# Mixture-of-experts loop on one core: a shared TensorE block for 64 and 96 rows, the 128-row body set apart, the split item reordered, the second weight sum made before an expert's early items

## The reference, cut to what matters

```python
def expert_block(args):
    e, tok, gt = args
    xb = hf[tok]
    g = xb @ w_gate[e] + b_gate[e]
    u = xb @ w_up[e] + b_up[e]
    g = jnp.minimum(g, SWIGLU_LIMIT)
    u = jnp.clip(u, -SWIGLU_LIMIT, SWIGLU_LIMIT)
    act = (u + 1.0) * (g * jax.nn.sigmoid(g * SWIGLU_ALPHA))
    y = act @ w_down[e] + b_down[e]
    return y * gt[:, None].astype(y.dtype)
```

## Time and profile before

| | us |
|---|---|
| median of three runs (lowest, highest) | 2254.84 (2250.0, 2255.2) |
| the profiled execution's own time | 2249.11 |
| its span, first to last instruction | 2247.3 |
| TensorE matmul busy | 2097.6 |
| VectorE busy | 1229.5 |
| ScalarE busy | 647.5 |
| mean granted TensorE clock | 0.975 |

### The profile page before, as it was taken

How to read it: one execution, slowest core, us unless ns; L and a number is a source line. 1 busy time by engine, 2 the same in 40 slices (tenths; PEclk the granted TensorE clock), 3 DMA queues, 4 the chain that set the end, 5 groups by cost and what they waited for, 6 DMA issues and landing times.

```text
span 2247.3 us, 35366 instructions
## 1 busy us (share of the span) xinstructions
PE 2097.6 (93%) x11374; PEld 911.6 (41%) x11375; DVE 1229.5 (55%) x2403; ACT 647.5 (29%) x1252; POOL 567.1 (25%) x537
## 2 busy tenths in 40 slices
PE   8999999977999799899898999979998999999997
PEld 6546676433333333333333334323332333333343
DVE  4323996776573563277263546526643576556753
ACT  2001886122322332222223232212222222222332
POOL 3271124133221221221222213211212122122223
PEclk9999999988999899999999999989999999999998
DMA  8002000246688569389859667765889868677674
GB/s 308 20 16 88 28 1 6 90 167 239 223 286 313 186 224 323 125 288 325 318 172 338 241 244 246 247 240 181 306 297 352 306 226 284 226 248 246 234 253 183
DMA packets 151941, 485.70 MB, mean 216 GB/s; under 512 B 20288, under 2 KB 37973, under 8 KB 151310
## 3 DMA queue, kind: packets, MB, share of 16 engines
q1 hardware_dynamic: 116192, 444.81, 52.5%
q0 software_dynamic: 33792, 34.66, 8.1%
q10 hardware_dynamic: 1874, 5.02, 0.6%
HBM read 461.26 MB, written 43.09 MB: 224 GB/s over the span
## 4 chain that ended last, share of the span: by engine, by line
PE 89%; issue 4%; DVE 2%; ACT 2%; DMA 1%; POOL 1%; DVEq 1%; ACTq 0%; POOLq 0%
PE psum L2283 24%; PE psum L2312 15%; PE psum L2079 14%; PE psum L1718 6%; PE psum L2125 5%; PE psum L1824 4%; PE psum L1857 3%; PE psum L1817 3%; PE psum L1714 2%; PE psum L2005 2%; PE psum L2066 2%; PE psum L2137 1%; PE psum L1866 1%; PE psum L2307 1%; PE psum L2290 1%
## 5 line engine op out<-in xcount | busy, mean ns | idle before, releaser
L774 POOL DMA_INDIRECT residual_rows<-work x184 | 330.5, 1796 | 584.5 <-ACT work L994 534.4
L2312 PE MATMUL psum<-weights,work 128*128 128x512 f32 x736 | 326.8, 597 | 26.0 <-ACT work L1024 26.0
L2079 PE MATMUL psum<-weights,work 128*64 128x512 f32 (+2 forms) x1536 | 308.3, 607 | 36.0 <-issue 36.0
L2283 PE MATMUL psum<-x,work 128*64 128x512 f32 x1472 | 331.7, 598 | 3.6 <-DVE work L1554 3.6
L1547 DVE TENSOR_TENSOR x<-weights 128x2048 f32<-128x2048 f32 x92 | 206.7, 2289 | 112.0 <-PE psum L2290 73.9
L2283 PE MATMUL psum<-weights,work 128*64 128x512 f32 x1104 | 250.6, 596 | 0.0
L731 POOL DMA_INDIRECT work<-normed_rows,work x47 | 51.6, 1098 | 713.1 <-PE psum L2005 520.9
L1404 DVE SCALAR_TENSOR_TENSOR work<-psum,work 128x4 f32<-128x4 f32 x47 | 7.4, 158 | 402.3 <-PE psum L1998 402.3
L2312 PEld LDWEIGHTS psum<-weights,work 128*128 128x128 f32 x736 | 136.2, 190 | 189.5 <-issue 189.5
L1547 DVE TENSOR_TENSOR x<-weights,x 128x2048 f32<-128x2048 f32 x92 | 208.2, 2284 | 0.4 <-DMA weights<-in_w_up 0.4
L2079 PEld LDWEIGHTS psum<-weights,work 128*64 128x64 f32 (+2 forms) x1536 | 97.6, 133 | 226.1 <-issue 223.9
(11 more groups left out here) (302 smaller groups left out, 2694.0 us busy)
## 6 DMA issues: line engine op xcount, KB each, us to landing
weights<-in_w_gate SPq DMA_DIRECT2D x64, 2048.0 KB, 8.0
weights<-in_w_up SPq DMA_DIRECT2D x64, 2048.0 KB, 13.6
weights<-in_w_down SPq DMA_DIRECT2D x64, 2048.0 KB, 8.6
residual_rows<-x SPq DMA_DIRECT2D x9, 512.0 KB, 2.9
normed_rows<-work ACTq DMA_DIRECT2D x9, 512.0 KB, 2.8
x<-in_x SPq DMA_DIRECT2D x8, 512.0 KB, 9.0
weights<-in_w_in SPq DMA_DIRECT2D x16, 256.0 KB, 9.3
weights<-in_w_in SPq DMA_DIRECT2D x8, 512.0 KB, 11.8
```

Of the source, the lines that this page charges most:

```text
L774: pl.indirect_dma_start(acc_d[:, :], bass.IndirectOffsetOnAxis(dest[:, b:b + 1], 0), yrow[:, b * BLK:(b + 1) * BLK], None, bounds_check=UN ...
L2079: mm = pe.matmul(out.rearrange("p (m n) -> p m n", m=2), xT[:, k, lo:lo + cols], wgu[:, :, k, blk * BLK:(blk + 1) * BLK], start=(k == 0), ...
L2283: mm = pe.matmul(out, tokens[:, k, :], weights[:, :, k, g * BLK:(g + 1) * BLK], start=start and k == 0, stop=ends and k == 3)
L2312: mm = pe.matmul(bank(4 + h), actT[:, k, :], wdn[:, k, h * HALF:(h + 1) * HALF], start=False, stop=(k == DT - 1))
```

## The change

On TensorE the bodies for 64 and 96 rows are cut in three: a first part of each (its waits, for 96 rows the third unit's first half, and `own_places`), then a common block `experts_halves` (both halves of units 0 and 1, the next rows, `index`, biases), then an end of each. The body for 128 rows is emitted ahead of `experts_next`, outside the stretch of the loop's other blocks. In the split item the bias of bank 3 starts its group instead of ending it, in both places; `transposes(2)` goes ahead of `row_transposes(1)`; `transposes(3)` goes ahead of the fourth pair of down products. On VectorE `weight_sum(1)` moves from the split item to the expert's start, behind `weight_sum(0)`, with its wait for `s_wk[1]`.

```diff
@@ -1580,10 +1580,6 @@
...
                 split_token_sum(3)
-                dve.wait_ge(s_wk[1], 32 * e + 32)
-                dve.wait_ge(s_wts, 8 * n + (WTS0 + 2))
-                weight_sum(1, 0)
-                weight_sum(1, 1)
                 dve.wait_ge(s_prod, 3 * n + 2)
@@ -1625,6 +1621,11 @@
...
                     weight_sum(0, 1)
+                    n = dve.value_load(splits[0:1, bass.ds(e, 1)], min_val=0, max_val=EXPERTS)
+                    dve.wait_ge(s_wk[1], 32 * e + 32)
+                    dve.wait_ge(s_wts, 8 * n + (WTS0 + 2))
+                    weight_sum(1, 0)
+                    weight_sum(1, 1)
                 run_early(begin, stop)
@@ -2000,10 +2001,10 @@
...
-                for c in range(4):
-                    k = 4 * q + c
-                    mm = pe.transpose(bank(7, P, c * P), xg[:, k * P:(k + 1) * P], ident[:, :])
-                mm.then_inc(s_xtp, 1)
+                all_four = [pe.transpose(bank(7, P, c * P), xg[:, (4 * q + c) * P:(4 * q + c + 1) * P], ident[:, :])
+                            for c in range(4)]
+                all_four[-1].then_inc(s_xtp, 1)
+                return all_four
@@ -2083,18 +2081,18 @@
...
-                    for s in range(1 if tokens == 32 else 2):
-                        mm = pe.transpose(bank(6, P, s * P), hid[:, b, s * P:(s + 1) * P], ident[:, :])
-                    return mm
+                    return [pe.transpose(bank(6, P, s * P), hid[:, b, s * P:(s + 1) * P], ident[:, :])
+                            for s in range(1 if tokens == 32 else 2)]
...
-                    if tokens in (64, 96):
+                    if tokens == 64:
...
-                            mm = pe.matmul(PS[64 * h:64 * h + 64, 4 * HALF:5 * HALF], onesb[rows_of(h), 0:64],
-                                           brow_dn[rows_of(h), :], start=True, stop=False)
+                            pe.matmul(PS[64 * h:64 * h + 64, 4 * HALF:5 * HALF], onesb[rows_of(h), 0:64],
+                                      brow_dn[rows_of(h), :], start=True, stop=False)
+                        return
@@ -2175,14 +2173,11 @@
...
-                units = 2 if tokens == 32 else {64: 2, 96: 3, 128: 4}[tokens]
-                pe.wait_ge(s_xT, 2 * j + 1)
-                pe.wait_ge(s_wk[0], 32 * e + 32)
-                pe.wait_ge(s_hid, UNIT * j + UNIT)
-                pe.wait_ge(s_aTm, UNIT * j + 1)
-                for b in range(units):
-                    mm = gate_up(b, range(4))
-                mm.then_inc(s_k03, 1)
+                def item_waits():
+                    pe.wait_ge(s_xT, 2 * j + 1)
+                    pe.wait_ge(s_wk[0], 32 * e + 32)
+                    pe.wait_ge(s_hid, UNIT * j + UNIT)
+                    pe.wait_ge(s_aTm, UNIT * j + 1)
@@ -2190,74 +2185,104 @@
...
-                    row_transposes(q)
...
+                    return row_transposes(q)
...
+                def place_waits():
+                    pe.wait_ge(s_idxb, j + 2)
+                    pe.wait_ge(s_found, 2 * j + 2)
...
+                def bias_waits():
+                    pe.wait_ge(s_chosen, j + 1)
+                    pe.wait_ge(s_yr, UNIT * j + UNIT)
...
+                def gate_up_ends(b, last=False):
+                    gate_up(b, range(4, DT)).then_inc(s_gu, UNIT - b if last else 1)
...
+                def hidden(b, last=False):
+                    transposes(b)[-1].then_inc(s_htp, UNIT - b if last else 1)
...
+                def next_item():
+                    pe.reg_load(next_tokens, items[0:1, bass.ds(j + (TABLE + 1), 1)])
+                    pe.reg_load(loaded_expert, items[0:1, bass.ds(j + 1, 1)])
+                    pe.reg_alu(next_expert, loaded_expert, 0, ALU.max)
+                    pe.reg_load(third_expert, items[0:1, bass.ds(j + 3, 1)])
...
+                if part == "places":
+                    item_waits()
+                    if tokens == 96:
+                        gate_up(2, range(4))
+                    place_waits()
+                    own_places()
+                    return
+                if part == "halves":
+                    gate_up(0, range(4))
+                    gate_up(1, range(4)).then_inc(s_k03, 1)
+                    rows(0)
+                    bias_waits()
+                    index(j + 2)
+                    bias(0)
+                    bias(1)
+                    down_bias()
+                    pe.wait_ge(s_wk[1], 32 * e + 32)
+                    gate_up_ends(0)
+                    gate_up_ends(1)
+                    return
+                if tokens == 64:
+                    next_item()
+                    next_rows()
+                    both = transposes(0)
+                    both[0].then_inc(s_gu, UNIT - 2)
+                    both[1].then_inc(s_htp, 1)
+                    rows(1)[0].then_inc(s_biased, 1)
+                    down_64(0, 0)
+                    hidden(1, True)
+                    down_64(0, 1)
+                    down_64(1, 0).then_inc(s_d03, 1)
+                    down_64(1, 1).then_inc(s_dps, 1)
+                    return
+                if tokens == 96:
+                    bias(2)
+                    down_bias()
+                    next_rows()
+                    hidden(0)
+                    gate_up_ends(2, True)
+                    next_item()
+                    hidden(1)
+                    rows(1)
+                    down_64(0, 0)
+                    down_64(0, 1)
+                    hidden(2, True)
+                    down_64(1, 0)
+                    down_64(1, 1)
+                    down_rest().then_inc(s_dps, 1)
+                    return
...
+                units = 2 if tokens == 32 else UNIT
+                item_waits()
+                for b in range(units):
+                    mm = gate_up(b, range(4))
+                mm.then_inc(s_k03, 1)
...
-                pe.wait_ge(s_aTm, UNIT * j + 1)
-                pe.wait_ge(s_idxb, j + 2)
-                pe.wait_ge(s_found, 2 * j + 2)
-                pe.wait_ge(s_chosen, j + 1)
-                pe.wait_ge(s_yr, UNIT * j + UNIT)
+                place_waits()
+                bias_waits()
...
-                def gate_up_ends(b):
-                    gate_up(b, range(4, DT)).then_inc(s_gu, 1 if b < units - 1 else UNIT - b)
...
-                def hidden(b):
-                    transposes(b).then_inc(s_htp, 1 if b < units - 1 else UNIT - b)
...
-                def next_item():
-                    pe.reg_load(next_tokens, items[0:1, bass.ds(j + (TABLE + 1), 1)])
-                    pe.reg_load(loaded_expert, items[0:1, bass.ds(j + 1, 1)])
-                    pe.reg_alu(next_expert, loaded_expert, 0, ALU.max)
-                    pe.reg_load(third_expert, items[0:1, bass.ds(j + 3, 1)])
...
+                gate_up_ends(0)
+                gate_up_ends(1, tokens == 32)
...
-                    gate_up_ends(0)
-                    gate_up_ends(1)
...
-                    hidden(1)
+                    hidden(1, True)
...
@@ -2284,11 +2309,11 @@
...
-                def bias(to, h, ends):
+                def bias(to, h, first):
...
-                                       start=False, stop=ends)
+                                       start=first, stop=not first)
@@ -2324,7 +2349,8 @@
...
-                bias(1, 0, True).then_inc(s_prod, 1)
+                bias(1, 0, False).then_inc(s_prod, 1)
+                bias(3, 1, True)
@@ -2332,8 +2358,8 @@
...
                 for k in range(4):
-                    product(3, a12, wgt_half(1, 1), k, True, False)
-                bias(3, 1, True).then_inc(s_gu, 1)
+                    mm = product(3, a12, wgt_half(1, 1), k, False, True)
+                mm.then_inc(s_gu, 1)
@@ -2357,13 +2383,12 @@
...
                 pe.wait_ge(s_yr, UNIT * j + UNIT)
+                pe.wait_ge(s_u, 7 * n + (UNIT0 + 1))
                 for h in range(2):
-                    mm = pe.matmul(bank(4 + h), onesb[rows_of(h), :], brow_dn[rows_of(h), :], start=True, stop=False)
-
-                pe.wait_ge(s_u, 7 * n + (UNIT0 + 1))
-                summed(3, 3, a22, True, False)
-                bias(3, 1, True).then_inc(s_gu, 1)
-                pe.sem_inc(s_biased, 1)
+                    pe.matmul(bank(4 + h), onesb[rows_of(h), :], brow_dn[rows_of(h), :], start=True, stop=False)
+                bias(3, 1, True).then_inc(s_biased, 1)
+
+                summed(3, 3, a22, False, True).then_inc(s_gu, 1)
                 pe.reg_load(next_tokens, items[0:1, bass.ds(j + (TABLE + 1), 1)])
@@ -2371,15 +2396,15 @@
...
                 transposes(1)
+                transposes(2)
                 pe.wait_ge(s_seen, j + 1)
                 row_transposes(1)
-                transposes(2)
                 pe.wait_ge(s_wk[2], 16 * e + 16)
                 pe.wait_ge(s_aTm, UNIT * j + 4)
-                for k in range(4):
-                    mm = down(k)
-                mm.then_inc(s_d03, 1)
+                for k in range(3):
+                    down(k)
                 transposes(3)
```

(49 more changed lines are left out.)

31 lines of the change are left out of this document (1 added, 30 removed).

## The result

The changed kernel takes 2194.78 us in the median of four runs (2189.23 to 2195.3); the kernel before 2254.77 (2250.0 to 2255.2) beside it. The ratio is 0.9733, interval 0.9713 to 0.9754: 60 us faster, outside my 2202 to 2244 on the fast side. The profiled execution took 2195.29 us, its span is 2193.5, so the spans differ by 53.8 us. The other 6 of 60: the profiled execution of before lay 5.7 under its median, that of after lies within 0.5 of its own.

A forecast was written before the change was run, and what follows sets the result against it. TensorE's unbroken line of matmuls in the item loop was taken as the bound. Code size 25, split item 14.5 and weight_sum(1) -1.5 gave 38 us off the 2254.8 median: 2217 us, own range 2203 to 2232, 8-in-10 range 2202 to 2244.

The forecast's parts named there:

- weight_sum(1): VectorE's second weight sum, 4.5 us, moved to the expert's start: 2.5 us gained behind early 32-row items, net -1.5 us.
- the large term: Code size in the item loop: the loop fits eight instruction blocks, issue gaps behind the first passes go, 25 us net.
- the biases: Split item on TensorE: biases only change places, one change of type less at 0.1 each, 1 to 2 us.
- the time given back to late transfers: Item entry at 1701: an earlier start doesn't bring weights earlier, so 6.14 and 2.2 of clock are lost, -8.3 us.
- the second wait: Split item: TensorE's second 0.56 us wait for ScalarE's copy goes in each of 23 items, 13 us.
- the new entries: A branch and six register instructions for each of 30 entries, mostly hidden: -3 us, bounds 0 and -25.
- The gaps and their clock: TensorE's issue gaps at item entries go, 46.5 us, and the lower clock behind five of them, 9 us.
- The first pass and the last item: First pass: one load more and low clock, -10 us; last item: 128-row body's first block loaded again, -7 us.
- The first wait stays: Split item: the first 0.56 us wait stays, since transposes(2) starts only when its bank is free; bounds +2 and -5.
- the first (gaps stay): Rival: loop still doesn't fit or gaps have another cause; only the split item's 14.5 less 1.5 gained, 2242; chance 0.13.
- The second (thrash): Rival: instruction blocks thrash and the 30 new jumps load too, 2335, or 2272 with a third loading; chance 0.07.
- The third (VectorE late in every early item): Rival: weight_sum(1) ends after find_places was due, 2 us lost in each of 15 early items, 2246; chance 0.06.

The follow-up runs named there:

- 129 instructions inside: The changed kernel with 129 never-entered instructions between the bodies of 32 and 64 rows, inside the loop: 2190.25 us, ratio 0.9727.
- 257: The changed kernel with 257 never-entered instructions between the bodies of 32 and 64 rows, and one more branch test for 128 rows: 2249.17 us, ratio 0.999.
- the kernel moved by 169 instructions: The changed kernel with 169 never-entered instructions ahead of the 128-row body, outside the loop: 2295.81 us, ratio 1.0191.

## Why the prediction was wrong

The mechanism of the large term held: the gaps were code loads, and they went when the loop fitted. Several terms of the sum were mis-sized, two of them because their mechanism was wrong (the biases and the weight sum), and I carried an offset over that was chance. The steps that failed, in the order of their size: `weight_sum(1)` (-1.5 forecast, -8.8 measured), the offset of 6 us, the biases (1 to 2, measured 7.4), the time given back to late transfers (8.3, measured 2.7), the second wait (0.56 an item, measured 0.80), the new entries (3, measured 0). All but the first made the kernel faster than forecast, so the first hid a part of the miss, which is luck. By the spans of before (2247.3), the split item's three steps alone (2223.9), the changed kernel with the sum back (2182.7) and the changed kernel (2193.5):

| | predicted, us | measured, us |
|---|---|---|
| code size and placement | 25 | 41.2 |
| split item | 14.5 | 23.4 |
| `weight_sum(1)` | -1.5 | -10.8 |
| profiled executions | 38 | 53.8 |

Single spans carry some 3 us of low-clock stretches each, so the terms below go by items. The 16 us that the first row lacks lie for the most part in the costs that I set against the gaps, not in the gaps. To this come 6 us of the offset: I carried the 5.7 us between before's profiled execution and its median over to after, whose profiled execution lies 0.5 above its median. The median of before was 2249.6 to 2253.4 beside the experiments, so that offset was chance.

- **The gaps and their clock** (55.5 us forecast, 46.5+9). Nearly right: the eight items of 96 rows and the three of 64 behind them lost 52.4 us, and 8 packets moved past 524 us where I gave 10 to 12.
- **Given back at the item behind the single 64-row item** (8.3 for the transfer, 3.5 for the weight sum, so 11.8). The sum nearly fits, with 10.1 measured, but by luck. The division is wrong: against the three reorderings alone, the item with the sum back is 2.7 us longer, and the sum's place costs 8.8. I let the earlier start be eaten by the transfer and then priced the sum by a transfer that "doesn't move"; in the trace the second half landed 12.3 us behind the item's start, for 7.6 before. The 2 us at the item of 733 did occur in kind: its down product, which had no such wait before, stands 1.18 us for the second down half. The item is only 0.76 us longer, since before it began at the lower clock:

```profile
752.44 1.93 PE L2147 MATMUL psum<-weights,work 128*32 128x256 f32 x32 [1.18 <-DMA weights<-in_w_down]
```

- **The first pass and the last item** (10 and 7). Measured 7.5 (5.7 of later start and 1.75), and 6.1, of which 2.9 is clock that some other kernels with the same wait don't show.
- **New entries** (3, bounds 0 and 25). No cost: undisturbed 64-row items are 0.10 us shorter than before.
- **The second wait in the split item** (0.56 by 23). A step that failed: I took the listed idle time for the cost. It is 0.80, since 0.16 of overlap with the next matmul goes with it, and 0.06 in the down matmuls whose cause is open: 0.24 by 23, 5.5 us.
- **The first wait stays.** Right: 1.91 us from transposes to down product in both kernels. The sign I gave (23 waits of 0.56) came out as 23 of 0.26 and a rest of 0.13, with the same time.
- **The biases** (1 to 2). Wrong in kind: "only change places" overlooked that two pairs on different rows of the array run together. 0.32 by 23, 7.4 us.
- **`weight_sum(1)`**: the 2.5 us behind early 32-row items (forecast as gain) is not there, and the loss at the item behind the single 64-row item is 8.8 and not 3.5, since all of VectorE's token sums stand behind the late transfer.

Of the rivals, the first (gaps stay) did not happen but is less than a block of dead code away: 129 instructions inside do nothing, 257 bring it back with 2249 us, where I had given 2242. The second (thrash) has its time in the kernel moved by 169 instructions, 2296 between the 2272 and 2335 that I gave, but not its mechanism: there the new jumps, places to halves (L2463) and halves to ends (L2469), take at most 192 and 235 ns, and the stalls of up to 7543 ns are at the branches that pick the next item (L2443). My reading of the margin, "69 instructions in front and about 120 behind", holds: the changed kernel stands 66 behind a block's start and 143 before its eighth block. The third (VectorE late in every early item) did not occur. 46 branches back of at most 186 ns, over seven blocks, refute the second at this size.

The Trainium skill, Runtime: NRT & Kernel Launch, section Instruction fetch mechanics, whose two lines and forced fetches were weighed there, is not borne out by these rows where it speaks of two lines; the page works those out from 32 KiB by 16 KiB, and 32 KiB is the size that it gives for engines other than TensorE. Its 128 KiB for TensorE, eight blocks, agrees with the runs.

## What to carry to other kernels

Count the blocks of 256 instructions that a loop on TensorE touches, not the instructions: shorten or move the code until no more than seven are touched (all ten kernels here with seven ran without the gaps, all eight with more had them), and look at the branch's longest duration and at the packets of the instruction queue, since a few instructions anywhere ahead of the loop can cost 5%. Price a wait by the distance between starts with and without it and not by its listed idle time. A wait on a late transfer must stand behind all work of its engine that doesn't need it.

## What the runs showed of the hardware that I had not expected

- TensorE's instruction room is used up by where the loop lies: 24 never-executed instructions fewer ahead of it made the kernel 105 us slower (2190.89 to 2295.81 us), with stalls of up to 18.8 us.
- Half a fix can be worse than none: taking the 128-row body out of the loop, with the loop still touching eight blocks by my count, went from 64 packets to 70 and from 2250 to 2285 us.
- Four bias matmuls of 32 rows by 64 columns, on four different groups of rows, took 0.41 us together, as long as two.
- A wait of 0.56 us on TensorE, removed whole, gave 0.80 us back.
